# Expert matrices loaded in two halves of neighbouring rows instead of four quarters

## What is computed

```
def expert_block(args):
    xb, e = args
    g = xb @ w_gate_e[e] + b_gate_e[e]
    u = xb @ w_up_e[e] + b_up_e[e]
    g = jnp.minimum(g, SWIGLU_LIMIT)
    u = jnp.clip(u, -SWIGLU_LIMIT, SWIGLU_LIMIT)
    act = (u + 1.0) * (g * jax.nn.sigmoid(SWIGLU_ALPHA * g))
    return act @ w_down_e[e] + b_down_e[e]
```

## Time and profile before

| | us |
|---|---|
| median of 3 runs | 1339.21 |
| the runs, lowest and highest | 1338.64, 1341.05 |
| span of the profiled execution, first to last instruction | 1338.2 |
| PE busy in it | 1246.2 (93%) |
| PE weight loads | 558.5 (42%) |
| DVE, ACT, POOL busy | 262.6, 229.1, 10.6 |
| bytes moved | 453.01 MB, 339 GB/s over the span |

### The profile page before, as it was taken

How to read it: one execution, slowest core, us unless ns; L and a number is a source line. 1 busy time by engine, 2 the same in 40 slices (tenths; PEclk the granted TensorE clock), 3 DMA queues, 4 the chain that set the end, 5 groups by cost and what they waited for, 6 DMA issues and landing times.

```text
span 1338.2 us, 14530 instructions
## 1 busy us (share of the span) xinstructions
PE 1246.2 (93%) x5484; PEld 558.5 (42%) x5484; DVE 262.6 (20%) x573; ACT 229.1 (17%) x466; POOL 10.6 (1%) x20
## 2 busy tenths in 40 slices
PE   7499999999899999989899999999898999999996
PEld 6358888886433333323232323223232323232332
DVE  4300745152411111111111111111111111111112
ACT  3023334100201111111111111111111111111113
POOL 1000000000000000000000000000000000000000
PEclk9799999999999999999999999999999999999998
DMA  7733663465399999999999999999999999999994
GB/s 197 179 137 126 251 252 126 157 224 181 142 351 409 410 410 410 410 410 409 410 410 410 410 410 410 410 410 410 409 410 410 410 410 410 410 410 410 409 409 158
DMA packets 132924, 453.01 MB, mean 339 GB/s; under 512 B 10588, under 2 KB 12742, under 8 KB 132902
## 3 DMA queue, kind: packets, MB, share of 16 engines
q1 hardware_dynamic: 132902, 452.71, 87.1%
HBM read 450.06 MB, written 2.62 MB: 338 GB/s over the span
## 4 chain that ended last, share of the span: by engine, by line
SPq 52%; PE 35%; DMA 5%; issue 4%; DVE 3%; ACT 1%; ACTq 0%
SPq L307 49%; PE bank L1053 13%; PE bank L1217 13%; PE bank L1059 4%; DMA w_down_sb<-in_w_in 3%; SPq L346 2%; DMA w_up_sb<-in_w_up_e 1%; DVE arena L824 1%; PE bank L1332 1%; DMA w_down_sb<-in_w_out 1%; SPq L358 1%; PE bank L1089 1%; PE bank L1106 0%; PE bank L1231 0%; DVE arena L743 0%
## 5 line engine op out<-in xcount | busy, mean ns | idle before, releaser
L1217 PE MATMUL bank<-w_down_sb,arena 128*64 128x512 f32 x1024 | 238.4, 603 | 40.1 <-DMA w_down_sb<-in_w_down_e 39.5
L1217 PE MATMUL bank<-arena 128*64 128x512 f32 x1032 | 243.3, 598 | 0.0
L1217 PE MATMUL bank<-w_up_sb,arena 128*64 128x512 f32 x1024 | 235.7, 598 | 7.5 <-DMA w_up_sb<-in_w_up_e 7.1
L1053 PE MATMUL bank<-arena,w_down_sb 128*128 128x256 f32 x1024 | 225.8, 382 | 2.4 <-DMA w_down_sb<-in_w_in 1.2
L1053 PEld LDWEIGHTS bank<-arena,w_down_sb 128*128 128x128 f32 x1024 | 195.0, 191 | 30.6 <-DMA w_down_sb<-in_w_in 1.6
L1217 PEld LDWEIGHTS bank<-w_down_sb,arena 128*64 128x64 f32 x1024 | 68.7, 137 | 205.8 <-issue 128.4
L1217 PEld LDWEIGHTS bank<-w_up_sb,arena 128*64 128x64 f32 x1024 | 67.7, 136 | 148.7 <-issue 120.3
L1217 PEld LDWEIGHTS bank<-arena 128*64 128x64 f32 x1032 | 71.4, 137 | 135.4 <-issue 135.4
L1217 PE MATMUL bank<-w_gate_sb,arena 128*64 128x512 f32 x512 | 116.7, 598 | 0.0
L991 DVE TENSOR_SCALAR arena<-bank 128x512 f32<-128x512 f32 x32 | 22.1, 692 | 315.2 <-PE bank L1217 315.2
L988 DVE TENSOR_TENSOR arena<-arena 128x512 f32<-128x512 f32 x32 | 22.1, 692 | 301.7 <-ACT arena L617 301.7
(11 more groups left out here) (225 smaller groups left out, 574.6 us busy)
## 6 DMA issues: line engine op xcount, KB each, us to landing
w_up_sb<-in_w_up_e SPq DMA_DIRECT2D x128, 1024.0 KB, 18.2
w_down_sb<-in_w_down_e SPq DMA_DIRECT2D x128, 1024.0 KB, 18.4
w_gate_sb<-in_w_gate_e SPq DMA_DIRECT2D x64, 1024.0 KB, 18.0
arena<-in_w_gate_e SPq DMA_DIRECT2D x64, 1024.0 KB, 18.5
w_down_sb<-in_w_in SPq DMA_DIRECT2D x14, 2048.0 KB, 8.8
w_down_sb<-in_w_proj_rnn SPq DMA_DIRECT2D x2, 2048.0 KB, 8.1
w_down_sb<-in_w_proj_att SPq DMA_DIRECT2D x2, 2048.0 KB, 7.7
w_down_sb<-in_w_out SPq DMA_DIRECT2D x2, 2048.0 KB, 8.9
```

The costliest lines, as they stand in the source:

```text
L1053: ins = eng.matmul(ps[:, n * T:(n + 1) * T], w[:, k, (2 * b + n) * P:(2 * b + n + 1) * P], rhs[:, k, :], start=(k == 0), stop=(k == KC - 1))
L1217: ins = eng.matmul(ps[b * JB:(b + 1) * JB, :], lhsT, w[:, h * CH:(h + 1) * CH], **flags)
```

## The change

The constant `NQ` goes from 4 to 2, and a new `KQ = KC // NQ` is 4, the blocks of one part. Three things follow.

- A matrix is loaded with two transfers of 2 MiB where there were four of 1 MiB, and PE waits for, and signals, halves.
- Within a half, partition p takes the four neighbouring rows 4p to 4p + 3, one stretch of 16 KB in memory, where it took two single rows of 4 KB, 128 rows apart. Block k of half q holds rows 512q + 4p + (k mod 4).
- The transposes of tokens and activation take every fourth column to match (`every_fourth`), at a step of 16 bytes.

The between-step of a contraction stays ahead of block 6, and the early loads of expert 0 stand behind two chunks, 4 MiB behind each, and no longer behind four with 2 MiB each.

```
-NQ = 4
+NQ = 2
+KQ = KC // NQ
...
                 rows = D // NQ
-                src = w[0][expert, q * rows:(q + 1) * rows, :].rearrange("a (k p) n -> p (a k) n", p=P)
-                eng.dma_start(place[:, q * KC // NQ:(q + 1) * KC // NQ, :], src).then_inc(loaded[m][q], 16)
+                src = w[0][expert, q * rows:(q + 1) * rows, :].rearrange("a (p k) n -> p (a k) n", p=P)
+                eng.dma_start(place[:, q * KQ:(q + 1) * KQ, :], src).then_inc(loaded[m][q], 16)
...
+            def every_fourth(src, c):
+
+                return src.rearrange("s (p c) -> s c p", c=KQ)[:, c, :]
+
             def turn_gather():
                 for c in range(4):
-                    ins = eng.transpose(bank[2][:, c * P:(c + 1) * P], xg[:, c * P:(c + 1) * P], ident[:, :])
+                    ins = eng.transpose(bank[2][:, c * P:(c + 1) * P], every_fourth(xg, c), ident[:, :])
...
                 for q in range(NQ):
-                    if q == NQ - 1 and between is not None:
-                        between()
                     eng.wait_ge(arrived[q], count)
-                    for k in (2 * q, 2 * q + 1):
+                    for k in range(q * KQ, (q + 1) * KQ):
+                        if k == KC - 2 and between is not None:
+                            between()
                         ins = pair(ps, block_of(xgT[parity], k), w[:, k, :], start=(k == 0), stop=False)
                     ins.then_inc(used[m], 1)
...
                     for c in range(4):
-                        ins = eng.transpose(bank[1][:, c * P:(c + 1) * P], av[:, c * P:(c + 1) * P], ident[:, :])
+                        ins = eng.transpose(bank[1][:, c * P:(c + 1) * P], every_fourth(av, c), ident[:, :])
...
                 for q in range(NQ):
                     eng.wait_ge(loaded["down"][q], j * 16 + 16)
-                    for k in (2 * q, 2 * q + 1):
+                    for k in range(q * KQ, (q + 1) * KQ):
                         ins = pair(bank[3], block_of(avT, k), WD[:, k, :], swap=parity, start=(k == 0), stop=(k == KC - 1))
```

## The result

The changed kernel takes 1305.82 us (median of 4 runs, 1304.55 to 1308.37) against 1338.93 for the kernel before (4 runs, 1338.37 to 1341.05): a ratio of 0.9748, with a 95% interval from 0.9735 to 0.9762. The forecast, 1326.6, had the direction and little over a third of the gain, and its range ended 0.2 us above the median.

The account below looks back on a forecast made before the run. The prediction took the expert stage's transfers at full DMA engines as the bound: span 1338.2 - 15.0 (fewer pieces) + 2.4 (coarser parts at the end) = 1325.6, shown as 1326.6 us; range 1306 to 1344.

Parts of the forecast that it names:

- What bounds the kernel: Experts' steady stage: the transfers at 409.6 GB/s set 61.44 us per two jobs, PE having 5.6 us in hand.
- ahead of that neither holds for long: Slices before 13: claimed that neither full DMA engines nor a granted clock of 9 tenths or more lasts there.
- 3.7 ns each: Expert matrix transfers: price per piece; 12 fewer pieces give 416.9 GB/s and save 15.0 us over 14 pairs.
- The cost of the coarser parts: Waits for halves: +2.4 us at the end, where block 4 waits for the last up matrix; 0 at the start.
- the 0: Start of the run-time expert loads: halves are issued later, but larger parts fill the engines' holes, costing 0.
- The prediction's worst case: Start of the run-time expert loads: halves freed one quarter later would cost at worst 1.8 us.
- The strided transposes: PE's transposes of every fourth column: claimed to cost nothing, bounded by nothing and a doubling.
- my upper bound: Strided transposes doubling in time: 0.6 us per four, 3.5 us for the 6 groups behind the last wait.
- The cost per transfer: Rival, chance 0.20: expert transfers also have a fixed cost each, halving their number gives 423 GB/s and 1313.7 us.
- The rate that stays: Rival, chance 0.22: expert loads stay at 410 GB/s, leaving only the grain: 1341.6 us, up to 1345.
- the rate that falls: Rival, chance 0.08: engines reading 64 KB apart meet in memory, expert loads drop to 400.3 GB/s: 1361.6 us.
- PE didn't become the bound: Rival, chance 0.05: slower transposes or a falling clock make PE bound the expert stage, up to 1375 us.

Follow-up runs that it names:

- the first experiment: Changed kernel with rows 128 apart and plain transposes as before, only the two 2 MiB halves per matrix kept (4 KB pieces): 1342.97 us, ratio 1.0023 to the kernel before.
- the second experiment: Kernel before, still four 1 MiB transfers per matrix, with two neighbouring rows per partition (8 KB pieces) and every-second-column transposes: 1312.8 us, ratio 0.9803.

## Why the prediction was right or wrong

**What bounds the kernel** was right: in the changed kernel and in all eight experiments, as in the kernel before, the steady stage takes the time that the transfers take, whatever PE does. The frame of the sum, 14 pairs times the difference of a pair plus what happens at two ends, holds too: 14 x (61.44 - 58.73) = 37.9 us, and the last up matrix lands 37.3 us earlier. One reading of the rows was wrong without an effect on the sum: "ahead of that neither holds for long" is true of the engines, but the granted clock is 9 tenths or more in eleven of the first twelve slices too.

**The step that failed** is the one that worked out "3.7 ns each" for a piece, from 400.3 GB/s for pieces of 2 KB in three stretches of the mixer, and from it 2515.4 ns per MiB and 15.0 us. The mechanism was the forecast's own, fewer pieces; the size of the term was off by a factor of 2.5: a piece costs 9.4 ns, and 14 pairs saved 37.9 us, not 15.0. In steady stages the four sizes of piece measure, per MiB and engine (the pair's time by 24 MiB, times 1000):

| piece | pieces per MiB and engine | us per pair | ns | step, ns per piece |
|---|---|---|---|---|
| 2 KB | 32 | 65.05 | 2710 | |
| 4 KB | 16 | 61.44 | 2560 | 9.4 |
| 8 KB | 8 | 59.63 | 2485 | 9.4 |
| 16 KB | 4 | 58.73 | 2447 | 9.4 |

Twelve pieces fewer save 113 ns, not 45. I had taken four-microsecond windows behind an idle time for the steady rate, and the steady rate was in none of them. The rate for 4 KB, in contrast, came from pairs over 614 us.

**The cost of the coarser parts** was right at the end. From block 4 to block 6 it is 1220.68 - 1218.13 = 2.55 us, against 2.4; and the grain alone measured 2.7 us by the medians. At the start the 0 was slightly too low. The changed kernel moved 342 x 16 + 402 x 14 = 11,100 KB from 370 to 400 us (windows below: POOL busy, clock, DMA share, GB/s), against 5392 + 14 x 409.6 = 11,126 in the prediction's working for the kernel before. But full engines of the changed kernel would have moved 14 x 428.5 = 5999 KB in the second window, and they moved 5628: the holes weren't all filled, and 0.9 us is lost there. It fits the landing, which gains 37.3 us and not 37.9. In the first experiment the landing is 2.2 us later than before (1257.65 for 1255.45), of which its first scatter has 0.9 already (430.96 for 430.11), so there the start costs 1.3 us. The prediction's worst case was 1.8.

```profile
370.00:386.00 16.00, 0.00 (x0) 1.00 0.90 342
386.00:400.00 14.00, 0.00 (x0) 1.00 0.98 402
```

**The strided transposes** cost something, a sixth of my upper bound: a weight load 209 ns for 141, and 0.68 us instead of 0.59 to the next matmul. Six groups behind the last wait make 0.5 us, which with the 2.4 gives the 3.0 found there. My reason for taking nothing, that a column load isn't at the limit of reading, doesn't hold: a step of 16 bytes adds 48%, and the step of 8 bytes of the second experiment gives 207 ns, nearly the same. The Trainium skill (SBUF — State Buffer, on cachelines under the port swizzle) says that each access that crosses to another 16-byte line pays a penalty, and the trace agrees at the step of 16 bytes. By the same note two accesses to a line should go at full speed; at the step of 8 bytes the measurement differs, and decides.

**The rivals.** The cost per transfer, which I gave 0.20 and which came nearest in time, doesn't exist in what these runs can tell: 1 and 2 MiB agree at 4 and at 8 KB, 2 and 4 MiB at 16 KB. It had been fitted to the same false equation. The figure of the Trainium skill that I set beside it (HBM Reference, Specifications, about 425 GB/s for a core alone) was within 1% of the measured 428.5, and better than my working. The rate that stays and the rate that falls are refuted by the 428.5 GB/s of the changed kernel. PE didn't become the bound; it has 2.5 us per pair left.

**The range** fell short by 0.2 us: its low end was tied to the middle of a rival, and the highest microsecond of the trace, 430 GB/s, which I had named as a bound, would have put it at 1300.8 (1338.2 - 40.8 + 2.4 + 1.0).

None of the versions that compute the same beats the changed kernel. Pieces of 32 KB would need eight neighbouring rows per partition. If the price of a piece held there too, they would save 2 x 9.4 ns of 2447, an estimate of 0.45 us per pair; the tokens lie in two halves of the partitions and would have to be turned in twice as many transposes, for which PE has 2.5 us per pair. This wasn't tried.

## What to carry to other kernels

When a stage is bound by transfers at full engines, count the pieces that a partition's share falls into: each of them had a fixed price here, and what decides is the stretch that is contiguous on both sides, not the size of the transfer nor how near the rows lie to each other. A price for it has to come from a stretch in the steady state; the first microseconds behind an idle time read too fast here. And taking 4.4% off the time of the resource that bounds a stage gave 2.5% of the kernel, as the stage is two thirds of it and coarser parts take a little back at its end.

## What the runs showed of the hardware

- A transfer's piece costs 9.4 ns of the engine that moves it, with pieces from 2 to 16 KB, and the rest is 2560 - 16 x 9.4 = 2409.6 ns for 65,536 B, or 435.2 GB/s over all. The Trainium skill gives just this as the ceiling of the fabric (DMA: Bandwidth & Descriptors, Where 436 GB/s comes from). The Trainium skill's account of small descriptors (the same page, Why small descriptors are slow) has a fixed overhead of about 3 cycles per packet, which at the 850 MHz of the fabric is 3.5 ns, an estimate from the page's figures; the runs show 9.4 ns per piece.
- A piece has to be contiguous in memory and in the partition. Rows that are neighbours in memory but land apart count as pieces of their own: 61.44 us per pair and not 58.73. So do rows that land side by side but lie apart in memory, 61.44 in the first experiment.
- Behind an idle time, pieces of 2 KB moved at 406 GB/s for four microseconds, and then at 385. Why isn't shown.
- A weight load of 128 float32 columns at a step of 8 or 16 bytes takes 207 or 209 ns, and 141 ns without a step.
- A wait of PE of 2.4 us can, but needn't, be followed by work at the clock's lower level. In the run with chunk-shaped loads a wait of 1.94 us, at 856.20, was followed by 24 records in 7.07 us, and one of 1.94 us, at 465.87, by 24 in the usual 5.37. With waits up to 1.4 us in the first experiment the granted clock was 1.00 throughout the stage.
